# Rotary turns as ScalarE copies between partition halves, without permutation products

## The reference

```python
proj = jnp.einsum('btd,dn->btn', n, w_in[l])
(gq, gk, gv, gz, gb, ga, aq, ak, av, iq, ik, iw, gate_a, gate_b) = jnp.split(proj, split_at, axis=-1)
y_gdn = _gdn_branch(gq, gk, gv, gz, gb, ga, conv_w[l], a_log[l], dt_bias[l], gdn_norm[l])
y_dsa = _dsa_branch(aq, ak, av, iq, ik, iw, rope_att, rope_idx, L)
merged = (jax.nn.sigmoid(gate_a) * (y_gdn @ w_branch_gdn)      # einsums in the reference
          + jax.nn.sigmoid(gate_b) * (y_dsa @ w_branch_dsa))

def _apply_rope(x, cos, sin):            # heads of 128 (aq, ak) or 64 (iq, ik)
    x1, x2 = x[..., :half], x[..., half:]
    return jnp.concatenate([x1 * c - x2 * s, x2 * c + x1 * s], axis=-1)

# _dsa_branch, for blocks of 128 queries
s = jnp.einsum('bqhd,bsd->bqhs', qi, ki)                 # index scores, 8 heads of 64
s = jnp.einsum('bqhs,bqh->bqs', jax.nn.relu(s), wi)      # one score for each key
_, idx = lax.top_k(s, 64)                                # the keys that a query sees
logits = q . k_sel * 128 ** -0.5                         # 8 heads, 2 key heads
o = softmax(logits) @ v_sel
```

## Time and profile before

| | |
|---|---|
| median of three runs | 1282.94 us (1282.8 to 1283.43) |
| span of the profiled execution | 1279.9 us |
| TensorE busy | 1264.1 us, 99% of the span |
| VectorE busy | 916.9 us, 72% |
| ScalarE busy | 692.9 us, 54% |
| GpSimd busy | 126.3 us, 10% |
| 96 to 186 us | the attention projection, where the change lies |

### The profile page before, as it was taken

The page is one execution under the profiler, slowest core; times in us unless marked ns, Lnnn a source line. Parts: engine busy times, 40 slices in busy tenths (PEclk is TensorE's granted clock), DMA queues, the critical chain, the costliest instruction groups (busy, mean ns, idle before and its releaser), DMA issues.

```text
span 1279.9 us, 23417 instructions
## 1 busy us (share of the span) xinstructions
PE 1264.1 (99%) x9094; PEld 1171.2 (92%) x9094; DVE 916.9 (72%) x1244; ACT 692.9 (54%) x1034; POOL 126.3 (10%) x113
## 2 busy tenths in 40 slices
PE   9999999999999999999999999999999999999998
PEld 7997999999989998879998988999888997999986
DVE  7886864878768774458634547999757777899954
ACT  5656365654445443344355546666547566766642
POOL 0000142000000000000000001222200000354310
PEclk9999999999999999999999999999999999999999
DMA  7552333411455555554553454555554444455562
GB/s 294 173 188 101 132 132 100 135 64 67 165 186 179 195 174 187 197 181 156 207 187 111 161 168 162 197 170 190 207 205 166 163 152 162 165 171 190 187 223 99
DMA packets 30313, 212.81 MB, mean 166 GB/s; under 512 B 3488, under 2 KB 3616, under 8 KB 5152
## 3 DMA queue, kind: packets, MB, share of 16 engines
q1 hardware_dynamic: 29088, 206.53, 47.0%
q0 software_dynamic: 1152, 5.24, 1.3%
HBM read 210.71 MB, written 1.05 MB: 165 GB/s over the span
## 4 chain that ended last, share of the span: by engine, by line
PE 90%; DVE 5%; ACT 3%; DMA 1%; issue 1%; DVEq 0%; SPq 0%; ACTq 0%
PE lin L526 55%; PE lin L630 22%; DVE wlo L507 1%; PE lin L2765 1%; PE aux L2498 1%; PE aux L2470 1%; PE lin L552 1%; PE lin L2199 1%; DVE ht L1420 1%; PE aux L2353 1%; ACT lm L1269 1%; PE aux L2426 1%; PE aux L2616 1%; ACT whi L500 0%; PE aux L2301 0%
## 5 line engine op out<-in xcount | busy, mean ns | idle before, releaser
L507 DVE TENSOR_TENSOR wlo<-raw,whi 128x2048 fp32r<-128x2048 f32 x186 | 441.5, 2377 | 192.1 <-ACT whi L500 191.8
L500 ACT CAST whi<-raw 128x2048 fp32r<-128x2048 f32 x192 | 365.1, 1905 | 195.4 <-DMA raw<-in_stream 163.5
L526 PE MATMUL lin<-xhi,whi 128*128 128x256 f32 (+1 forms) x1584 | 451.7, 285 | 0.0
L526 PE MATMUL lin<-xlo,whi 128*128 128x256 f32 (+1 forms) x1584 | 447.6, 283 | 0.0
L526 PE MATMUL lin<-xhi,wlo 128*128 128x256 f32 (+1 forms) x1584 | 445.3, 281 | 0.0
L526 PEld LDWEIGHTS lin<-xhi,wlo 128*128 128x128 f32 x1584 | 299.4, 189 | 0.0
L526 PEld LDWEIGHTS lin<-xhi,whi 128*128 128x128 f32 x1584 | 297.3, 188 | 2.0 <-issue 0.8
L526 PEld LDWEIGHTS lin<-xlo,whi 128*128 128x128 f32 x1584 | 297.9, 188 | 0.3
L2168 DVE SCALAR_TENSOR_TENSOR ft<-fy,par,ft 128x254 f32<-128x254 f32 (+1 forms) x176 | 102.9, 623 | 5.9 <-DVE ft L2168 0.2
L526 PE MATMUL lin<-whi,xhi 128*128 128x256 f32 (+1 forms) x336 | 96.9, 288 | 0.0
L526 PE MATMUL lin<-wlo,xhi 128*128 128x256 f32 (+1 forms) x336 | 94.4, 281 | 0.0
(11 more groups left out here) (451 smaller groups left out, 2005.4 us busy)
## 6 DMA issues: line engine op xcount, KB each, us to landing
raw<-in_stream SPq DMA_DIRECT2D x193, 1024.0 KB, 5.0
gp<-in_gains POOLq DMA_DIRECT2D x6, 512.0 KB, 3.9
c<-in_const SPq DMA_DIRECT2D x1, 1460.0 KB, 16.3
h<-in_x SPq DMA_DIRECT2D x2, 544.0 KB, 4.5
c<-in_const POOLq DMA_DIRECT2D x1, 1024.0 KB, 6.0
ht<-in_xtok POOLq DMA_DIRECT2D x1, 1024.0 KB, 8.8
out<-ht SPq DMA_DIRECT2D x1, 512.0 KB, 2.6
out<-ht SPq DMA_DIRECT2D x2, 256.0 KB, 2.0
```

Source lines behind the costliest of these rows:

```text
L500: nc.scalar.copy(whi[:, s0 % 4], raw[:, s0 % 4]).then_inc(hi_ready, 1)
L507: nc.vector.tensor_tensor(wlo[:, s0 % 4], raw[:, s0 % 4], whi[:, s0 % 4].bitcast(F32), ALU.subtract).then_inc(lo_ready, 1)
L526: ins = nc.tensor.matmul(out, a, b, start=start and n == 0, stop=stop and n == 2)
```

## The change

ScalarE writes a second tile beside each projected tile, with the two halves of each head exchanged (`ikr`, `iqr`, `akr`, `aqr`), straight from PSUM, as copies from one range of partitions to another: four copies of 32 partitions for heads of 64, two of 64 partitions for heads of 128. The signs move into the sine table. The permutation products and their tables are gone. VectorE multiplies the exchanged tile by the sine table, in SBUF and in place, the tile by the cosine table, and adds; the exchanged ik also gets the `rstd` factor. In place of the bank VectorE waits for the pair (`pair_done`), which is freed after the exchanged copies. The first gate slot is computed whole in front of the logits of block 0, and these follow in one piece. GpSimd's low halves of slots 22 and 23 wait for `rope` 8 instead of 9.

```diff
@@ GpSimd
-            pool.wait_ge(S("rope"), 9)
+            pool.wait_ge(S("rope"), 8)
             pool_low(pool, FIRST["gb"] + 1, FIRST["gb"] + 3)
@@ ScalarE
+        def swapped(dst, src, half):
+            for lo in range(0, P, 2 * half):
+                mid, end = lo + half, lo + 2 * half
+                nc.scalar.copy(dst[lo:mid], src[mid:end])
+                ins = nc.scalar.copy(dst[mid:end], src[lo:mid])
+            return ins
...
             nc.scalar.copy(ik[:], PS[0][:, 0, 0:T1])
+            swapped(ikr, PS[0][:, 0, 0:T1], 32)
             nc.scalar.copy(smf[0:24], PS[0][0:24, 1, 0:T1]).then_inc(pair_free[0], 1)
...
-                    nc.scalar.copy(ak[:], PS[u % 2][:, :, 0:T1]).then_inc(pair_free[u % 2], 1)
+                    nc.scalar.copy(ak[:], PS[u % 2][:, :, 0:T1])
+                    swapped(akr, PS[u % 2][:, :, 0:T1], 64).then_inc(pair_free[u % 2], 1)
...
-                    dst = iq if name == "iq" else aq
-                    nc.scalar.copy(dst[:, 2 * j:2 * j + 2], PS[u % 2][:, :, META:T1]).then_inc(pair_free[u % 2], 1)
+                    dst, turned, half = (iq, iqr, 32) if name == "iq" else (aq, aqr, 64)
+                    x = PS[u % 2][:, :, META:T1]
+                    nc.scalar.copy(dst[:, 2 * j:2 * j + 2], x)
+                    swapped(turned[:, 2 * j:2 * j + 2], x, half).then_inc(pair_free[u % 2], 1)
@@ VectorE
             nc.vector.tensor_tensor(ik[:], ik[:], rstd[:], ALU.mult)
+            nc.vector.tensor_tensor(ikr[:], ikr[:], rstd[:], ALU.mult)
...
-                b = full(dve, name)
-                is_free(nc.vector.tensor_tensor(ctmp[:, 0, 0:n, 0:W], wide(b[:, 0:n * W], W),
-                                                bc(cst(sn, lo=t0, n=W), n), ALU.mult), name)
-                after(dve, name)
+                pair_done(dve, u)
+                nc.vector.tensor_tensor(turned, turned, bc(cst(sn, lo=t0, n=W), n), ALU.mult)
                 own.link(nc.vector.tensor_tensor(x, x, bc(cst(c, lo=t0, n=W), n), ALU.mult))
-                nc.vector.tensor_tensor(x, x, ctmp[:, 0, 0:n, 0:W], ALU.add).then_inc(S("rope"), 1)
+                nc.vector.tensor_tensor(x, x, turned, ALU.add).then_inc(S("rope"), 1)
@@ TensorE
-                b = fill(name)
-                for n in range(x.shape[1]):
-                    ins = nc.tensor.matmul(b[:, n * W:n * W + W], turn, x[:, n], start=True, stop=True)
-                is_full(ins, name)
...
-            gate_part(0, 0, 2)
-            rotation(8)
-            gate_part(0, 2, 5)
+            gate_part(0, 0, 8)
             pe.wait_ge(S("rope"), 9)
-            logits(0, 0, 4)
-            gate_part(0, 5, 6)
-            logits(0, 4, 6)
-            gate_part(0, 6, 7)
-            logits(0, 6, 8)
-            gate_part(0, 7, 8)
+            logits(0, 0, 8)
```

More of the change, by code:

```diff
@@ L70 @@
 CONST1 = [("ident", 128), ("window", 32), ("upper", 128), ("upper16", 128), ("ones16", 128), ("spread", 128), ("head", 8),
-          ("levels", 4 * 128), ("cosa", T1), ("sina", T1), ("cosi", T1), ("sini", T1), ("turna", 128),
-          ("turni", 128), ("past", 2 * T1)]
+          ("levels", 4 * 128), ("cosa", T1), ("sina", T1), ("cosi", T1), ("sini", T1),
+          ("past", 2 * T1)]
 CONST2 = [("rcos", SEQ), ("rsin", SEQ), ("decay", 4 * SEQ), ("past2", 2 * SEQ)]
@@ L213, in program @@
         irelu = at("irelu", B + 74112, [P, 4, T1])
+        ikr = at("ikr", B + 66496, [P, T1])
+        akr = at("akr", B + 67584, [P, 2, T1])
+        iqr = at("iqr", B + 78464, [P, 4, SEQ])
+        aqr = at("aqr", B + 82560, [P, 8, SEQ])
         zs = at("zs", B + 76288, [P, 8, SEQ])
@@ L389, in use_next @@
                 turn_at[0] += 1
-        ROT = ["rot_ik", "rot_iq0", "rot_iq1", "rot_ak0", "rot_ak1"] + [f"rot_aq{n}" for n in range(4)]
         for step in PROJECT:
-            if step[0] == "rot":
-                use_next(ROT[step[1]])
-            elif step[0] == "idx":
+            if step[0] == "idx":
                 use_next(*[f"idx{step[1]}_{hh}" for hh in range(4 * step[2], 4 * step[2] + 4)])
@@ L398, in program @@
                 use_next({"l2": "l2sum"}.get(step[0], step[0]))
-        use_next(ROT[8])
         for t in range(2):
@@ L1529, in rotate @@
             def rotate(step):
-                name, x, W, c, sn, t0 = todo[step]
+                x, turned, u, W, c, sn, t0 = todo[step]
                 n = x.shape[1]
-                b = full(dve, name)
-                is_free(nc.vector.tensor_tensor(ctmp[:, 0, 0:n, 0:W], wide(b[:, 0:n * W], W),
-                                                bc(cst(sn, lo=t0, n=W), n), ALU.mult), name)
-                after(dve, name)
+                pair_done(dve, u)
+                nc.vector.tensor_tensor(turned, turned, bc(cst(sn, lo=t0, n=W), n), ALU.mult)
                 own.link(nc.vector.tensor_tensor(x, x, bc(cst(c, lo=t0, n=W), n), ALU.mult))
-                nc.vector.tensor_tensor(x, x, ctmp[:, 0, 0:n, 0:W], ALU.add).then_inc(S("rope"), 1)
+                nc.vector.tensor_tensor(x, x, turned, ALU.add).then_inc(S("rope"), 1)
                 dve.wait_ge(S("rope"), step + 1)
@@ L1973, in rotations @@
         def rotations():
-            yield "rot_ik", ik[:].unsqueeze(1), T1, "cosi", "sini", 0
+            yield ik[:].unsqueeze(1), ikr[:].unsqueeze(1), 0, T1, "cosi", "sini", 0
             for n in range(2):
-                yield f"rot_iq{n}", iq[:, 2 * n:2 * n + 2], SEQ, "cosi", "sini", META
+                a = slice(2 * n, 2 * n + 2)
+                yield iq[:, a], iqr[:, a], pair_first["iq"] + n, SEQ, "cosi", "sini", META
             for n in range(2):
-                yield f"rot_ak{n}", ak[:, n:n + 1], T1, "cosa", "sina", 0
+                a = slice(n, n + 1)
+                yield ak[:, a], akr[:, a], pair_first["ak"], T1, "cosa", "sina", 0
             for n in range(4):
-                yield f"rot_aq{n}", aq[:, 2 * n:2 * n + 2], SEQ, "cosa", "sina", META
+                a = slice(2 * n, 2 * n + 2)
+                yield aq[:, a], aqr[:, a], pair_first["aq"] + n, SEQ, "cosa", "sina", META
         def dve_second(dve, own):
@@ L2213, in pe_body @@
             is_full(ins, "small_t")
-            todo = list(rotations())
             def project(name, j):
@@ L2304, in pe_body @@
             for step in PROJECT:
-                if step[0] == "rot":
-                    rotation(step[1])
-                elif step[0] == "idx":
+                if step[0] == "idx":
                     index_scores(step[1], step[2])
@@ L2901, in constants @@
         ang = pos[None, :] * inv[i % (dim // 2)][:, None]
[L2902 to L2907, removed]
+        lower = (i % dim < dim // 2)[:, None]
+        c["cos" + tag], c["sin" + tag] = np.cos(ang), np.where(lower, -np.sin(ang), np.sin(ang))
     past = [np.where(pos[None, :] <= (META + t * P + i)[:, None], 0.0, -BIG) for t in range(2)]
```

## The result

The changed kernel takes 1296.45 us in the median of four runs (1295.95 to 1297.56), the kernel before 1283.18 in four: 1.0110 times as long, with a 95% interval of 1.0098 to 1.0123, so 13.3 us slower. Forecast were 1293.0 us, or 10.5 more. The sign and the mechanism of the largest term were right, the size was some 3 us short, and by the profiled executions (1295.0 against 1279.9) 4.6 us.

What follows compares the result with a forecast made beforehand. TensorE held 90% of the chain and VectorE 5%; 8.2 us for the held ninth rotation plus 1.5 and 0.8 for the clock made 10.5, and 1282.9 + 10.5 = 1293.4, taken as 1293, range 1283 to 1297.

Steps and rivals of the forecast that it cites:

- the largest term: At the ninth rotation: GpSimd's earlier start holds VectorE out twice, so the second logits come 8.2 us later.
- the shorter rotations: VectorE's rotations keep three instructions each but lose one semaphore wait, about 0.1 us each.
- GpSimd's exclusion: Ninth rotation: GpSimd's two 4.6 us low halves each block a VectorE instruction with two SBUF inputs; it ends 9.2 us later.
- The rivals of one hold and of none: Ninth rotation: GpSimd holds VectorE out only once, 1289 us, chance 0.13; or not at all, 1282.0 to 1283.6, chance 0.18.
- I take 0.46 each: ScalarE's added copies at the index-query pairs: 0.46 us from one to the next, bounds 0.2 and 0.9.
- the first place: About 100 to 117 us: ScalarE's added copies before two weight casts make the index scores 2.7 us later.
- I add 1.5 for the long gap, and half of 1.5 for the gap of 4.9: Clock lost in TensorE's gaps of 10.9 and 4.9 us: cold starts add 1.5 and 0.8 us.
- the short gap: TensorE's idle gap of 4.9 us before the index scores, priced at half a cold start of 1.5 us.
- The early convolution "at nothing": Extra small-slot copies and a VectorE product push the first convolution 1.5 us; counted as nothing, bound 0 to 0.5.
- The new order: Gate work before the logits: eight logits take 1.85 us, against 4.19 before for eight logits and three eighths of the gate slot.
- The base: Span 1279.9 us against median 1282.94: 3.0 us lie around the span, so changes of the span are added to the median.

Runs made afterwards that it cites:

- e11_after_fill_short: Changed kernel plus 24 useless warm-up products in TensorE's wait before the index scores and 44 in its wait for the ninth rotation; 1291.5 us.
- the warm kernel: Changed kernel with both long TensorE waits filled by 24 and 44 useless warm-up products, clock full behind them; 1291.5 us.
- e2_before_pool8: Kernel before, with only GpSimd's low halves of slots 22 and 23 waiting for eight rotations instead of nine; 1291.7 us, 1.0072.
- e6_order: Changed kernel with GpSimd back at nine rotations and gate slot and logits of block 0 in the old interleaved order; 1289.29 us, 1.0057.
- e1_pool9: Changed kernel with one number undone: GpSimd's low halves of slots 22 and 23 wait for nine rotations again; 1286.6 us, 1.0036.
- e3_low_behind: Changed kernel with GpSimd back at nine rotations and VectorE writing slot 17's low half behind the third rotation; 1283.94 us, 1.0013.
- e7_rearranged: Changed kernel with GpSimd at nine rotations, old logits order, and ScalarE's copies off the path to the scores; 1279.03 us, 0.9972.

## Why the prediction was right and where it failed

| where (us) | before | forecast | after |
|---|---|---|---|
| index scores start | 114.03 | 116.75 | 119.38 |
| rotation at 148.25 starts | 148.25 | 150.0 | 154.64 |
| ninth rotation ends | 166.0 | 176.65 | 180.38 |
| first product after ten logits | 170.98 | 181.5 | 185.22 |

The forecast of the last row is 170.98 and the 10.5 of the sum. There the kernel is 14.2 us late, 3.7 more than forecast, and the steps below add up to that: 1.35 arrive from before 96 us where nothing was put, ScalarE's copies cost 1.3 more, the clock 1.3 more, and small rests 0.7 more; the hold by GpSimd and the shorter rotations gave 0.9 back.

*GpSimd's exclusion: right.* Two instructions of VectorE, one for each of GpSimd's, the third ahead of them free. Held were 8.4 us, and the text had 9.2. So between rows two and three the table has 25.74 us measured for 26.65 forecast. The rivals of one hold and of none are ruled out by the rows 4.98 and 4.87.

*The step "I take 0.46 each": failed.* It was read from a copy followed by a cast that begins at the same partition, as none of the added copies does. At 0.58, eight copies are 1.0 us more, and the first place lost 4.0 instead of 2.7 (5.35 less the 1.35 that arrive from earlier). The range of 0.2 to 0.9 held it. Why the step is 0.58 is open in part, as said above.

*The step "I add 1.5 for the long gap, and half of 1.5 for the gap of 4.9": failed, by as much as the copies.* The two cost 2.0 and 1.6, so 3.6 and not 2.3; the short gap, put at half, cost a whole cold start in each of the six traces that have it unfilled (1.2 to 2.6 us). The row it came from was no good measure: the same 20 records at the start of the program take 3.89 us before and 4.64 after the change, so their time depends on the execution. And the windows of both traces give a granted clock of 1.00 there, so no row shows that they ran at the lower level. The Trainium skill (TensorE: Matmul & The Clock Gate, Part 1) says of the count of cold products at the start that it varies from run to run; the two rows vary too, but with a clock given as 1.00 they do not show that this is why.

*The early convolution "at nothing": failed.* VectorE's first convolution starts at 29.55 instead of 26.84, and TensorE waits 0.43 us for it, the only wait between 14 and 96 us, where before there was none. All in all 0.65 us, just outside the bound of 0.5. Another 0.7 of the 1.35 comes from the start-up: the sums behind the warm-up products begin 0.15 us later and take 4.47 us instead of 3.93. The edit touches neither, and a trace with the same start-up as the change (`e11_after_fill_short`) has 3.94, so this differs from execution to execution.

*The new order: right in sign.* 4.91 us before (166.07 to 170.98) against 2.78 in the warm kernel: 2.1 less, where 2.3 was reckoned.

*The base: failed.* "3.0 us lie around the span" was not so, and the "some 3 us" that stands ahead of the prediction neither. Where time and span are of one execution, 1.7 to 1.9 us lie between them (1296.74 less 1295.0 in the change). The 3.0 compare the span of one execution with the median of others, and the profiled one of before was one of the shorter ones of a program that takes 1281.2 to 1283.7. Adding a change of the span to that median hid 1.2 us of the miss.

Left open: why the clock falls in the second block in some executions (between 960 and 1000 us in the traces of the change and of six other kernels) and not in others (seven traces, that of before among them), and whether that makes the spread of the kernel before, 1281.2 to 1283.7; why it fell at 126 us in `e2_before_pool8`, behind waits of 0.5 us and less; and whether the first partition alone makes a copy 0.12 us dearer.

## What to carry to other kernels

Before moving GpSimd's work ahead in time, look at what VectorE does then: beside GpSimd instructions of 4.6 us here, a VectorE instruction with two SBUF operands waited one out whole, and an exchange of a PSUM operand for an SBUF one makes it such an instruction. Copies that take work off TensorE help only if nothing that TensorE waits for stands behind them: with GpSimd's start left at nine rotations, the kernel with the copies in front of two casts was 3.7 us slower than before, and with the path rearranged around them 3.8 faster, 5.2 with another order of the logits. And price a gap on TensorE not by its length alone but with the slower work behind it: fill it with products that do nothing and last as long as the gap.

## What the runs showed of the hardware

- The length of a gap alone did not tell whether TensorE's clock falls. It fell in all six unfilled gaps of 5.6 or 5.7 us and in one of 4.0 (`e6_order`), at the end of two gaps of 1.9 (`e1_pool9`, `e3_low_behind`), and not in one of 2.7 (`e7_rearranged`). One program (`e3_low_behind`) ran 1282.5 us at a mean granted clock of 1.000 and 1286.6 at 0.994. A cold start cost 1.2 to 2.6 us of dense products behind it.
- Ten useless products of 128x128 in float32 take 2.2 us at the full clock. Such products, 24 and 44 of them in the two waits of the changed kernel, kept the clock and gained 4.5 to 5 us.
- ScalarE's copies with 512 elements to a partition take 0.58 us for 32 partitions and for 64, and 0.55 to 0.59 for 128. The exchange between partitions does not make a copy longer (0.57 to 0.58 us either way). The step to the next copy was 0.46 to 0.48 us where both begin at partition 0, else 0.57 to 0.60.
- A low clock can hide another bound: from the logits to the next product took 4.60 us with the clock partly at 1.2 GHz and 4.60 at 2.4, since GpSimd's low half ended then.
- VectorE instructions of 0.69 us with two SBUF operands took 4.40 to 4.98 beside GpSimd's of 4.6, one for each; with one operand in PSUM, 0.69 beside the same.
